# A two-layer, two-block model on one core: TensorE's order of steps in the second block's mixers, and late projection columns in half steps

## The reference, cut to what matters

```
def second_block(x, p, norm_attn, w_in, w_out, ...):
    for i in range(DEPTH):
        a = rms_norm_2(h, norm_attn[i])
        u = a @ w_in[i]
        (nsa_q, k_cmp, v_cmp, k_slc, v_slc, k_win, v_win, nsa_g,
         d_q, d_k, d_v,
         g_q, g_k, g_v, g_lr, g_og,
         r_q, r_f, r_i, r_og) = split_cols(u, IN_SPLITS_2)
        o_a = nsa_attention(...)
        o_b = diff_attention(...)
        o_c = gla_mixer(...)
        o_d = hgrn2_mixer(...)
        mix = jnp.concatenate([o_a, o_b, o_c, o_d], axis=-1)
        h = h + mix @ w_out[i]
...
```

## Time and profile before

| | before |
|---|---|
| median of three runs | 2447.26 us |
| the profiled execution, its own time | 2453.92 us |
| its span | 2452.1 us |
| TensorE busy | 2393.8 us (98% of the span) |
| VectorE, ScalarE, GpSimd busy | 679.1, 457.5, 136.4 us |
| mean granted clock of TensorE | 0.989 |
| HBM read | 538.12 MB |

### The profile page before, as it was taken

The page is one execution under the profiler, slowest core; times in us unless marked ns, Lnnn a source line. Parts: engine busy times, 40 slices in busy tenths (PEclk is TensorE's granted clock), DMA queues, the critical chain, the costliest instruction groups (busy, mean ns, idle before and its releaser), DMA issues. The chain is left out here.

```text
span 2452.1 us, 49793 instructions
## 1 busy us (share of the span) xinstructions
PE 2393.8 (98%) x22691; PEld 1376.7 (56%) x22691; DVE 679.1 (28%) x1417; ACT 457.5 (19%) x781; POOL 136.4 (6%) x355
## 2 busy tenths in 40 slices
PE   9999999999999889999999899999999999999999
PEld 8755558756555666887455655445343534343444
DVE  3545523445624551111024532101010101101012
ACT  1522321422323451000024531000000000000001
POOL 4011000011001210000002200000000000000000
PEclk9999999999999999999999999999999999999999
DMA  7522343422335423444447127999999999999992
GB/s 242 164 87 88 104 136 122 160 87 79 112 115 148 136 71 122 158 140 169 146 126 202 54 76 281 395 408 377 391 384 381 367 399 394 404 375 390 395 369 95
DMA packets 194437, 542.43 MB, mean 221 GB/s; under 512 B 29200, under 2 KB 61360, under 8 KB 194224
## 3 DMA queue, kind: packets, MB, share of 16 engines
q1 hardware_dynamic: 180576, 536.82, 59.8%
q10 hardware_dynamic: 13344, 1.35, 0.5%
q0 software_dynamic: 304, 1.05, 0.1%
HBM read 538.12 MB, written 1.05 MB: 220 GB/s over the span
## 5 line engine op out<-in xcount | busy, mean ns | idle before, releaser
L405 PE MATMUL psum<-ring,hT 128*128 128x512 f32 (+3 forms) x1120 | 477.3, 575 | 6.0 <-ACT area L829 4.5
L2760 PE MATMUL psum<-ring,mix 128*32 128x448 f32 x4608 | 438.7, 539 | 0.2 <-DVE mix L3022 0.2
L405 PEld LDWEIGHTS psum<-ring,hT 128*128 128x128 f32 x1120 | 205.9, 190 | 206.4 <-issue 180.9
L2760 PEld LDWEIGHTS psum<-ring,mix 128*32 128x32 f32 x4608 | 148.8, 110 | 282.6 <-issue 280.8
L2375 PE MATMUL psum<-hT,ring 128*128 128x256 f32 x896 | 193.7, 379 | 0.0
L2375 PEld LDWEIGHTS psum<-hT,ring 128*128 128x128 f32 x896 | 170.1, 190 | 23.0
L710 PE MATMUL psum<-hT,ring 128*128 128x256 f32 x768 | 166.4, 379 | 0.0
L710 PEld LDWEIGHTS psum<-hT,ring 128*128 128x128 f32 x768 | 145.9, 190 | 20.7 <-issue 1.0
L3011 DVE TENSOR_TENSOR area<-area,psum 128x1344 f32<-128x1344 f32 x16 | 24.6, 1535 | 457.5 <-PE psum L2760 457.5
L2773 PE MATMUL psum<-area 128*32 128x256 f32 x2688 | 148.2, 379 | 0.9 <-DVE area L3013 0.9
L2760 PE MATMUL psum<-area,mix 128*32 128x448 f32 x1536 | 147.3, 539 | 0.0
(11 more groups left out here) (532 smaller groups left out, 2193.2 us busy)
## 6 DMA issues: line engine op xcount, KB each, us to landing
ring<-in_w_in_dram SPq DMA_DIRECT2D x88, 1024.0 KB, 5.1
ring<-in_moe_w_gate_dram SPq DMA_DIRECT2D x96, 896.0 KB, 7.0
ring<-in_moe_w_up_dram SPq DMA_DIRECT2D x96, 896.0 KB, 7.5
area<-in_moe_w_down_dram SPq DMA_DIRECT2D x112, 512.0 KB, 5.9
ring<-in_moe_w_down_dram SPq DMA_DIRECT2D x112, 512.0 KB, 6.3
area<-in_moe_w_gate_dram SPq DMA_DIRECT2D x32, 896.0 KB, 7.1
area<-in_moe_w_up_dram SPq DMA_DIRECT2D x32, 896.0 KB, 7.0
ring<-in_w_out_dram SPq DMA_DIRECT2D x16, 1024.0 KB, 5.0
```

Of the source, the lines that this page charges most:

```text
L405: last = nc.tensor.matmul(acc(g)[:, t, 0:d["n"]], lhs(kk, t), w[:, k, :], start=kk == 0, stop=kk == d["nk"] - 1)
L2760: last = nc.tensor.matmul(PS[32 * j:32 * j + 32, 3 * p + b, 0:PIECE].rearrange("p (m n) -> p m n", n=32), tokens(k, b), w[:, :, j, :], sta ...
```

## The change

Two edits. A fill step yields after every second block of the depth, so it is two instructions and there are 48 of them in a layer. And the three strings are new (the old ones had a common opening, 34 letters, that is gone):

```
-                        if k % 4 == 3:
+                        if k % 2:
...
-        TENSOR_PLAN = OPENING + "adfgfdgaafagafaagafaafagafgfafafaafagagffafagfg"
+        TENSOR_PLAN = "cfggffcgffdcnfnfcgfaffcggcfacffgffcfafcafdafffgffdgagfaaafafaaaggafaafffffgffaafaaffaafffgfffffagaffgfg"
```

More of the change, by code:

```diff
@@ L1731, in diff_map @@
             return TT[r, 5 + f // P, :], TT[r, 7 + f // P, :]
-        OPENING = "cgfencfgcfngcfvgcfagfccgfacgfdafca"
-        TENSOR_PLAN = OPENING + "adfgfdgaafagafaagafaafagafgfafafaafagagffafagfg"
-        SCALAR_PLAN = OPENING + "adfgdefaagafagfaagfaaafagaffagfafaafaagvffagfapgpfvgpp"
-        VECTOR_PLAN = OPENING + "adgdaagaagaagaaaagaagaaaagaagapgpgpp"
+        TENSOR_PLAN = "cfggffcgffdcnfnfcgfaffcggcfacffgffcfafcafdafffgffdgagfaaafafaaaggafaafffffgffaafaaffaafffgfffffagaffgfg"
+        SCALAR_PLAN = "fcfgfencgcngcafvgcgccgafcffgfdadgdfeaaafgafafgafagaafaaagcafffaagaafffaagvfagpgfpffavpgp"
+        VECTOR_PLAN = "cgncgcgcgacgcccggadacaadnadgagaaagagaaaagaagaaaagaagapgpgpp"
         def blended(plan, **parts):
```

## The result

The changed kernel takes 2437.35 us (median of 8 executions, 2434.64 to 2444.3), the kernel before 2449.86 beside it on the same chip (8 executions, 2447.07 to 2453.14). The ratio is 0.9949, with an interval of 0.9938 to 0.9960: 12.5 us faster, where 11.1 were forecast.

A forecast was written before the change was run, and what follows sets the result against it. TensorE, busy 98% of the span, was taken as the bound, leaving only its idle time and clock. Waits 7.3 plus clock 5.2 less gaps 1.4 gave 11.1 us, from median 2447.26 to 2436.2, range 2428.5 to 2444.5.

The forecast's parts named there:

- Term 1, the waits: TensorE's waits in both mixer stages: 13.6 us left a layer against 16.8 and 17.7, gaining 7.3 us in both.
- turn 0: TensorE's step that needs the exponentials of round 0: a new wait of 2.6 us, with only 1.3 of work before it.
- up to scores 1: Stretch where the compressed output must be scaled before scores 1: 2.2 us idle, where it was 0.9.
- differential heads: TensorE's wait for VectorE's chain from scores 1: shrinks from 1.8 us to 0.1, with 9.1 of work in front.
- turn 1: TensorE's step 7.6 us after the differential heads: 1.8 us idle, where it was 2.2.
- outs 1: TensorE's step right behind turn 1, waiting for a copy behind VectorE's round 2: 1.75 us idle, new.
- turn 2: TensorE's step that needs the exponentials of round 2: 1.6 us idle, where it was 0.3.
- Term 3, the gaps: Three TensorE gaps without releaser, 4.0 us, two at outs 1: 1.4 us of them taken to come back, bounds 0 and 4.0.
- Term 2, the clock: TensorE's low clock patches in the stages: 5.6 us a layer falls to 3.0, gaining 5.2 us in both.
- The clock stays up: Rival: with fill spread through the stage no low clock patch remains; gain 18.5 us, 2428.8; chance 0.15.
- As often low, and the gaps back: Rival: the clock falls as often as before and the gaps return; gain 3.3 us, 2444.0; chance 0.17.
- TensorE's feed becomes the bound: Rival: TensorE stops where units of small matmuls stand back to back, 20 us; 7.5 slower, 2454.8; chance 0.08.

The follow-up runs named there:

- e7: Changed kernel with two half fill steps moved from behind turn 2 to just ahead of it; 2440.94 us, 0.9959 of the kernel before.
- e1: Kernel before with the new order only up to scores 1, then the old order in half steps; 2449.13 us, 0.9994 of the kernel before.
- e2: Kernel before with the old order up to scores 1 and the new order behind it; 2440.59 us, 0.9960 of the kernel before.
- e3: Changed kernel with each pair of half fill steps put together as a whole step; 2444.68 us, 0.9978 of the kernel before.
- e4: Changed kernel with one gated unit and its output moved from behind scores 1 to ahead of turn 0; 2436.72 us, 0.9949 of the kernel before.
- e8: Changed kernel with a gated unit and half fill steps moved into waits at the turns and outs 1, two ScalarE drains earlier; 2435.83 us, 0.9945 of before.
- e6: Changed kernel with unused small matmuls added in the waits ahead of turn 0, scores 1 and turn 1; 2441.45 us, 0.9958 of the kernel before.
- e9: e8 with unused small matmuls added in the two waits at the stage's end; 2435.40 us, 0.9943 of the kernel before.

## Why the prediction was right

The sum came out at 11.1 forecast, 12.5 measured. The kind of gain was right, some waiting and some clock, and so was the order of size of both. That the total fits so closely is in part luck: the waits gave more than forecast, the gaps came back where little of them was expected, and the clock's part stood partly in other places.

**Only TensorE's order moves; the rest is the same work.** Held: ScalarE is busy 61.53 where it was 61.54, VectorE 63.65 where it was 62.73, with the same counts.

**Term 1, the waits.** The walk against what the two profiles of the changed kernel show, in us (the issue gaps inside the stage apart; before in layer 0):

| place | before | forecast | layer 0 | layer 1 | second, 0 | second, 1 |
|---|---|---|---|---|---|---|
| L1801 | 1.9 | 0.1 | 0.2 | 0 | 0.2 | 0 |
| normed heads | 0 | 0.9 | 0.8 | 0 | 0.8 | 0 |
| L1822 | 2.4 | 0 | 0 | 0 | 0 | 0 |
| turn 0 | 0 | 2.6 | 2.75 | 1.6 | 0 | 1.3 |
| up to scores 1 | 1.1 | 2.2 | 1.5 | 2.2 | 2.2 | 2.2 |
| differential heads | 1.8 | 0.1 | 0 | 0 | 0 | 0 |
| turn 1 | 2.2 | 1.8 | 1.7 | 1.7 | 1.7 | 1.7 |
| outs 1 | 0.9 (gap) | 1.75 | 2.1 | 2.1 | 2.1 | 2.1 |
| turn 2 | 0.3 | 1.6 | 1.05 | 0.2 | 0.3 | 0 |
| end of stage | 1.3 + 1.8 | 0.7 + 1.8 | 0.6 + 2.0 | 0.6 + 2.0 | 0.6 + 2.0 | 0.6 + 2.0 |
| sum | | 13.6 | 12.7 | 10.4 | 10.0 | 10.0 |

In layer 0 of the first profile every wait named in advance is there, each within 0.7, and no other of over 0.3 us with a releaser. In the other three stages the sum is 3.2 to 3.6 less than forecast, most of it at turn 0, turn 2 and (in layer 1) the first heads. Those rows are the step that was mis-sized. The walk had no low patch in it, and one that comes ahead of turn 0 makes TensorE arrive later there and wait less: not at all in the second profile's layer 0. From turn 1 on and at scores 1 the walk holds in all four stages within 0.7, but for turn 2.

**Term 3, the gaps.** 1.4 us were taken to come back, between 0 and 4.0. There are 1.2 in layer 0 and 2.1 in layer 1, so 3.3 (1.5 and 2.8 in the second profile): nearly all of the 4.0. They stand at other instructions (L1815, L2235, L2269) and at L2010 as before. Together, idle time fell by 7.9 us (34.5 to 26.5, and to 24.4 in the second profile), where 7.3 - 1.4 = 5.9 was the forecast. The gaps' term was mis-sized by 1.9 us, and the waits' more than made up for it. By the Trainium skill ("Runtime: NRT & Kernel Launch", section Instruction fetch mechanics) nothing of the kind would have come back; the trace doesn't agree, if fetching is what they are, and that stays open: no run here took away what they stand at.

**Term 2, the clock.** The size of 5.2 us was about right and the place half wrong. TensorE's busy time in the stages, at equal work, fell by only 1.9 us (198.91 to 197.02; 197.73 in the second profile). The patch behind turn 1 and outs 1 is there as forecast, in all four stages of the two profiles. The one behind turn 0 and scores 1 is there only in layer 0 of the first; in the other three stages the early patches begin within 1.3 us of the end of gaps of no releaser (0.83 and 0.92 in layer 1, 0.47 in the second profile's layer 0, 0.93 in its layer 1). And the prediction held that outside the stages there was nothing for this change to touch, but there lay another 2.3 us (86.9 to 84.7, and 83.4 in the second profile). In layer 1, 1.3 of its 2.5 are at the start of the output product, right behind the last two waits, of which the first shrank from 1.3 to 0.6; the other 1.1 are a shorter patch further on, ahead of the experts. That the shrunken wait did it is not shown: e7 has the same two waits at its end as the changed kernel, and its stretch behind layer 1 is 52.2, as long as before (52.4). Clock in all: some 4 to 5 us, of 12 to 15 in these profiles. The executions say about the same: the column in the table falls from 25.1 (46 executions) to 19.5 (8, and 5 once more), 5.6 less. By the Trainium skill ("TensorE: Matmul & The Clock Gate", section on the second HAM failure mode) the frequent micro-idles would have kept the gain near 0. Inside the stages the trace comes near to that (1.2 and 1.9 us), over the whole it doesn't.

**The rivals.** "The clock stays up" is refuted by the windows at 841 and 865. "As often low, and the gaps back" was nearly right on the gaps (3.3 of 4.0) and close on the clock inside the stages; its 3.3 us came out too small because it left out what lies behind the stages, and because the waits of three stages of four gave more. "TensorE's feed becomes the bound" wanted gaps of 6 us a layer; there are 1.2 and 2.1.

**What would show it.** The stages were to end at about 107 to 110 us and did at 111.1 and 112.4 (111.0 and 111.1 in the second profile). These bounds didn't follow from the prediction's own terms, by which (3.2 and 4.1 of waits, 2.6 of clock, less 0.7 of gaps a layer) the stages end at 111.0 and 111.3. The 5.6 us of low clock a layer, too, don't follow from the rows beside it, 1.6 twice and "as much again", which is 4.8 or 6.4. L1515 keeps its number in the changed kernel, since it stands ahead of the removed line; the prediction said L1514. The fear for the waits from turn 2 on, where one us of lateness would go to the end, did not come true: behind turn 2 there is only a gap (0.4 to 1.1 in the four stages), and at the end the last waits are as forecast.

**What the prediction did not see** came out in the runs. By its own terms the waits up to scores 1 went from 5.2 (1.9, 2.4, 0.9) to 5.8, so in waits little was to be had there. That was not drawn out of the walk, and e1's theory expected the opposite. e1 and e2 settle where the gain is, 1.1 and 9.7 us, and the clock's part goes with the second half (26.5 and 19.0 beside 25.1). Why the clock is lower for less time there is open: which of the half steps or waits does it was not taken apart, and in whole steps (e3, 26.9) it doesn't come. The double use of one piece of work explains e4 and e7, and part of e8: work moved into a wait leaves the place that it came from, and if that place covers another chain, the wait goes there.

## To carry to other kernels

Walk the new order place by place, releases included, and let each piece of work cover one wait only: a wait that the profile names is a gap, but the fill for it is taken from the cover of another. Compare two stretches of an order only with the work inside them counted (the xcounts show what moved), and look at the clock behind the stage as well as in it, over many executions and not in one profile: the same wait before the same product was followed by 7.1 us or by 8.8. Steps of half the length are worth having where an order is placed by hand, since here over half of the gain needed them.

## What the runs showed of the hardware

- The length of a wait of TensorE doesn't tell whether a stretch at the 1.2 GHz level follows. It is 0.50 behind the 2.75 at turn 0, and behind the pair of 1.71 and 2.09 at turn 1 and outs 1, but also begins within 1 us after single gaps of 0.83 and 0.92 (changed kernel, layer 1); it is the 2.4 GHz level behind the 1.82 in the kernel before and behind the 1.59, 0.62 and 1.60 from turn 0 to scores 1 in the changed kernel's layer 1. Behind one and the same wait of 2.0 ahead of the output product its first sixteen records took 7.1 us in five stages, 8.8 in six and 10.0 in one.
- A low stretch ahead of a wait can cost nothing: in the changed kernel's second profile TensorE came to turn 0 behind 5.49 us of slow fill and didn't wait there, and the stage was 111.0 long, against 111.1 with the wait of 2.75.
- The executions of one kernel differ by 4 to 16 us (e6 2438.18 to 2442.51, e9 2427.32 to 2442.89), and the mean granted clock with them (e9 0.996 to 0.988). A gain of under 4 us by a reorder could not be told from this in 6 executions, even where both stages were plainly shorter (e8).
- Gaps with no releaser, of up to 2.0 us, stand in or behind dense runs of small matmuls. They change place with the order, and their sum over the two stages with it: 4.0 before, 3.3 and 4.3 in the two profiles of the changed kernel, 1.0 in e2 and 1.6 in e3.
